# The gated recurrence moved between the last projection tiles, its norm squared on ScalarE and gated on VectorE

## The chip, the core and the metric

The kernel runs on one core of a Trainium2 chip. The metric is the device time of one execution in microseconds (us). Engines are named as in the profile: PE (TensorE; PEld is its weight load), DVE (VectorE), ACT (ScalarE), POOL (GpSimd), and SP, whose queue issues the loads. SBUF and PSUM are the on-chip memories; PSUM has eight banks of 512 fp32 columns.

## What is computed

One step of a one-layer streaming encoder on 1040 prompt tokens (16 meta tokens and 1024 frames) and 32 tokens of running streams, 1072 in all: an FFN with LayerNorm, a mixer, a second FFN. The mixer has two branches. One is a sparse attention: an indexer scores all keys, the 256 highest keys of each query are kept, then softmax. The other is a gated linear recurrence over four heads with a 128 x 128 state each. Shortened:

```
aq, ak, av, iq, ik, iw, bq, bf, bi, bg, ga, gb = split(h @ w_in)
oa   = sparse_attention(aq, ak, av, top-k of the indexer's scores (iq, ik, iw))
logf = log(lb + (1 - lb) * sigmoid(bf));  kk = (1 - lb) * sigmoid(-bf);  rq = silu(bq);  rv = bi
# recurrence, per head and block of tokens, b = cumsum(logf):
o    = tril(rq exp(b) (kk exp(-b))^T) rv + (rq exp(b)) S
S    = S exp(b_last) + (kk exp(b_last - b))^T rv
on   = o * rsqrt(mean(o^2) + eps) * g_norm;   ob = on * silu(bg)
h    = LN(alpha h + (sigmoid(ga) (oa @ wa) + sigmoid(gb) (ob @ wb)) @ wo)
```

All of it is fp32; a large product is done as three matmuls of split operands (`product3`: high x high, high x low, low x high).

## The kernel before

The program is a chain of stages. Activations lie transposed, features on the partitions and the 1072 tokens along the free side, in three chunks of 384, 384 and 304 columns.

**Index and project** (`index_and_project`). 43 tiles of 128 output columns of `w_in` are multiplied with h. A tile has three chunks, a chunk is 24 matmuls into one of four PSUM banks, and ACT drains it (`Projection.drain`). A tile's weights come by SP, ACT rounds them to the high part (`split_hi`, issued when the tile two earlier is drained), POOL subtracts (`split_lo`). While PE does so, DVE runs the indexer's search: after the scores, 31 rounds of counting and then the passes that mark the chosen keys (to L1272). DVE has nothing to do with the projections. The last 24 tiles (bi, bg, ga, gb) go through an SBUF buffer to a DRAM scratch (`spill`); aq, rq, ak, av and bf stay in SBUF.

**Mixers** (`mixers`), after a barrier. It starts with 21 transposes of ak, av and the cache, which DVE copies out of PSUM, and the split of the keys. Then each engine walks one list made by `pass_order`. Attention has ten blocks of eight heads, 80 units: seven blocks of 128 queries with 272, 400, ... 1040 keys, the 32 running tokens (288 keys), the first 128 frames (144 keys) and the 16 meta tokens. A unit n has the parts S (scores on PE, the distance penalty and row maximum on DVE, exp on ACT), T (PE turns the probabilities, ACT copies them out) and V (product with the values). S runs two units ahead. Q makes the queries of a block (ACT, DVE), X turns a block's output. The recurrence's parts are spread over the same list by a pace (`PACE`): g per head (`sums`: running sum of logf and its shifts, on DVE), e 32 times (exp of a quarter of a head on ACT into one of two buffers, a product on DVE), then for each of 13 blocks of 80 tokens and the 32 running tokens k, v (PE turns keys and values, ACT copies them), a (scores on PE, bound and mask on DVE), o (read-out on PE, copy on DVE), u (state update on PE, sum and product on DVE). At the end come four n, one per head: POOL squares the output, PE averages over the head's features with a matrix of ones (L1610), ACT takes the root (L1706), DVE the reciprocal and the product (L1863, L1865), POOL multiplies with the gate (L1482). Ahead of the list ACT makes the sigmoids and the logarithm (L1626 to L1635).

**Back** (`back`): output projections, LayerNorm, second FFN. It starts when the mixers' barrier is passed.

Within an engine the order is the program's. A wait on ACT or DVE holds everything behind it.

Of the kernel before, what the change touches and what calls it, by code (L numbers as in the profile page):

```python
# [22 lines left out]
P = 128  # L23
# [860 lines left out]
def score_columns():  # L884

    at, out = 0, {}
    for b in range(1, NB):
# [9 lines left out]
SPILLED = [(col, j, func) for col, m, func in ((C_BI, 4, ACT.Copy), (C_BG, 4, ACT.Silu), (C_GA, 8, ACT.Sigmoid),  # L897
                                               (C_GB, 8, ACT.Sigmoid)) for j in range(m)]
SP_BI, SP_BG, SP_GA, SP_GB = 0, 4, 8, 16


def index_and_project(c, block, dram, st, f, norm):
# [9 lines left out]
    tiles = [[(C_IQ + P * j, P, 0)] for j in range(4)] + [[(C_IK, P, 0)]]  # L912
    NI = len(tiles)
    tiles += [[(C_BF + P * j, P, 0)] for j in range(4)]
    tiles += [[(C_AQ + DH * j, DH, 0), (C_AQ + DH * (j + 4), DH, DH)] for j in range(4)]
    tiles += [[(C_AK, P, 0)], [(C_AV, P, 0)]]
    tiles += [[(C_BQ + P * j, P, 0)] for j in range(4)]
    NK = len(tiles)
    tiles += [[(col + P * j, P, 0)] for col, j, _ in SPILLED]
    NTL = len(tiles)  # L920
# [24 lines left out]
    k_hi, k_lo = c.k_hi, c.k_lo  # L945
    queries = QueryStack(c, "ix", c.q_stack, [(2 * j, 2 * j + 1) for j in range(4)])
# [6 lines left out]
    spilled = [sem(f"spilled{i}") for i in range(3)]  # L953
# [8 lines left out]
    index = {x[:3]: n for n, x in enumerate(units)}  # L962
    blocks = [(n, b, QB) for n, b in enumerate(range(1, NB))] + [(NB - 1, "s", DEC)]
# [6 lines left out]
    def _(sp):  # L970
# [17 lines left out]
        n_out = store_rows(sp, ki_tok, dram["new_kidx_p"], dram["new_kidx_s"], ki_out)  # L988
        for n in range(NI + 3, NTL):
            pr.load(sp, n)  # L990
        sp.wait_ge(ki_out, n_out)

    @block.gpsimd
    def _(pool):
        pr.split_lo(pool, 0)
        pr.split_lo(pool, 1)
        pr.split_lo(pool, 2)
        pr.split_lo(pool, 3)
        pool.iota(dist[:].bitcast(I32), [[-1, LP]], base=LP - P, channel_multiplier=1).then_inc(dist_set, 1)
        for n in range(4, NTL):  # L1000
            pr.split_lo(pool, n)

    @block.tensor
    def _(pe):
# [45 lines left out]
        for n in range(NI + EARLY // 3, NTL):  # L1050
            for i in range(3):
                pr.multiply(pe, n, i)

    @block.scalar
    def _(act):
# [31 lines left out]
        def drain(n, i):  # L1087
            m = n - NI
            if m < 4:
                pr.drain(act, n, i, c.y[:, m, :])  # L1090
            elif m < 8:
                pr.drain(act, n, i, c.aq[:, m - 4, :], scale=qscale[:, m - 4:m - 3])
            elif m < 10:
                pr.drain(act, n, i, c.ak if m == 8 else c.av)
            elif n < NK:
                pr.drain(act, n, i, c.rq[:, m - 10, :], ACT.Silu)
            else:
                m = n - NK
                pr.drain(act, n, i, c.y[:, 5 + m % 3, :], SPILLED[m][2])
# [12 lines left out]
        act.wait_ge(qs_set, 8)  # L1112
        for n in range(NI + EARLY // 3, NTL):
            m = n - NK
            if m == 0:
                act.wait_ge(ki_out, 48)
            if m >= 3:
                act.wait_ge(spilled[m % 3], 16 * (m // 3))
            for i in range(3):
                drain(n, i)  # L1120
            if m >= 0:
                pr.wait_drained(act, n)
                act.dma_start(c.spill[m], c.y[:, 5 + m % 3, :]).then_inc(spilled[m % 3], 16)
        for i in range(3):
            act.wait_ge(spilled[i], 16 * len(range(i, len(SPILLED), 3)))

    @block.vector
    def _(dve):
# [59 lines left out]

        dve.wait_ge(dist_set, 1)
# [67 lines left out]
        for n, b, rows in blocks:  # L1257
# [16 lines left out]
            settled()  # L1274


LOOK = 2
PACE = 1.22


def pass_order(att_blocks, n_rec):
# [9 lines left out]
    att = [("Q", 0)] + [("S", n) for n in range(LOOK)]  # L1291
    for n in range(units + 1):
# [978 lines left out]
```

## Time and profile before

| | us |
|---|---|
| median of 3 runs (lowest, highest) | 2945.52 (2942.11, 2946.82) |
| the profiled execution | 2947.6 |
| its span | 2945.9 |

| engine | busy us | share of the span |
|---|---|---|
| PE | 2730.8 | 93% |
| DVE | 1341.0 | 46% |
| ACT | 668.3 | 23% |
| POOL | 485.8 | 16% |

Times in the rows count from the span's start. The projections end near 1447 us, the mixers run from 1452 to 1862 us. PEclk is the clock that TensorE was granted, 1.00 for 2.4 GHz and 0.50 for 1.2 GHz; a value between is a stretch that had both. A matmul's duration overlaps the next one's, so what a run of them costs is read from the start of the first to the start of what follows.

### The profile page before, as it was taken

How to read it: one execution, taken by the hardware profiler on the slowest of the kernel's cores; microseconds unless marked ns; L12 is line 12 of the kernel's file. 1: busy time of each engine (PE TensorE's matmuls, PEld its weight loads, DVE VectorE, ACT ScalarE, POOL GpSimd, SP SyncE). 2: the span in 40 equal slices, each digit the busy share in tenths (PEclk: the TensorE clock that was granted, in tenths of full speed). 3: DMA queues.
4: the chain of work that ended last, by engine and by line, in shares of the span. 5: the costliest groups of instructions: out<-in, count | busy, mean ns of one | idle time of the engine just before them, and what ended most of it. 6: DMA issues, size and time to landing. Idle time of an engine off the chain costs nothing. (4 is left out here: it accounts for less than half of the span.)

```text
span 2945.9 us, 41396 instructions
## 1 busy us (share of the span) xinstructions
PE 2730.8 (93%) x16384; PEld 2628.7 (89%) x16384; DVE 1341.0 (46%) x2842; ACT 668.3 (23%) x1135; POOL 485.8 (16%) x175
## 2 busy tenths in 40 slices
PE   8999999999977999999779986799999999999996
PEld 7999999999967799999768974699799999999995
DVE  2333333333254689992165437455543333333335
ACT  3111111111143522221255533200421111111102
POOL 1122111111010011222100002111111111222212
PEclk9999999999988999999859987799999999999998
DMA  4111111111021011232200000522011111111101
GB/s 146 44 43 43 48 55 54 43 43 30 1 71 44 15 44 44 96 95 89 97 1 31 1 1 8 183 75 80 29 44 43 43 43 43 43 43 44 55 16 60
DMA packets 143708, 149.13 MB, mean 51 GB/s; under 512 B 19648, under 2 KB 130336, under 8 KB 143472
## 3 DMA queue, kind: packets, MB, share of 16 engines
q1 hardware_dynamic: 140144, 134.45, 14.8%
q10 hardware_dynamic: 3456, 13.17, 1.1%
q8 instruction: 76, 1.25, 0.2%
q14 instruction: 32, 0.26, 0.0%
HBM read 123.82 MB, written 23.79 MB: 50 GB/s over the span
## 5 line engine op out<-in xcount | busy, mean ns | idle before, releaser
L475 DVE TENSOR_TENSOR ffn_prod<-ffn_gate,ffn_psu 128x384 f32<-128x384 f32 x132 | 69.5, 527 | 799.9 <-ACT ffn_gate L385 793.6
L67 PE MATMUL ffn_psd<-ffn_hid_hi,ffn_dn_hi 128*128 128x384 f32 (+1 forms) x1056 | 353.9, 335 | 12.7 <-DVE y L500 10.9
L67 PE MATMUL ixp_ps<-h_hi,ixp_hi 128*128 128x384 f32 (+1 forms) x1032 | 339.9, 329 | 20.2 <-ACT y L877 11.5
L67 PE MATMUL ffn_psg<-h_hi,ffn_up_hi 128*128 128x384 f32 (+1 forms) x1056 | 346.4, 328 | 8.4 <-DVE ffn_up_lo L400 6.6
L500 DVE TENSOR_TENSOR y<-y,ffn_psd 128x384 f32<-128x384 f32 (+1 forms) x480 | 250.9, 526 | 217.2 <-PE ffn_psd L69 217.2
L385 ACT ACTIVATE ffn_gate<-ffn_psg 128x384 f32<-128x384 f32 x132 | 61.9, 469 | 1259.3 <-PE ffn_psu L69 1259.2
L67 PE MATMUL ffn_psu<-h_hi,ffn_up_hi 128*128 128x384 f32 (+1 forms) x1056 | 344.0, 326 | 0.0
L68 PE MATMUL ffn_psg<-h_lo,ffn_up_hi 128*128 128x384 f32 (+1 forms) x1056 | 343.9, 326 | 0.0
L69 PE MATMUL ffn_psd<-ffn_hid_hi,ffn_dn_lo 128*128 128x384 f32 (+1 forms) x1056 | 343.8, 326 | 0.0
L68 PE MATMUL ffn_psd<-ffn_hid_lo,ffn_dn_hi 128*128 128x384 f32 (+1 forms) x1056 | 343.7, 325 | 0.0
L69 PE MATMUL ffn_psg<-h_hi,ffn_up_lo 128*128 128x384 f32 (+1 forms) x1056 | 343.1, 325 | 0.0
L69 PE MATMUL ffn_psu<-h_hi,ffn_up_lo 128*128 128x384 f32 (+1 forms) x1056 | 343.0, 325 | 0.0
L68 PE MATMUL ffn_psu<-h_lo,ffn_up_hi 128*128 128x384 f32 (+1 forms) x1056 | 342.1, 324 | 0.0
L68 PE MATMUL ixp_ps<-h_lo,ixp_hi 128*128 128x384 f32 (+1 forms) x1032 | 337.9, 327 | 0.0
L69 PE MATMUL ixp_ps<-h_hi,ixp_lo 128*128 128x384 f32 (+1 forms) x1032 | 336.7, 326 | 0.0
L404 POOL TENSOR_TENSOR ffn_dn_lo<-ffn_dn_raw,ffn_dn_hi 128x2048 fp32r<-128x2048 f32 x22 | 101.8, 4627 | 912.5 <-ACT ffn_dn_hi L378 912.5
L400 POOL TENSOR_TENSOR ffn_up_lo<-ffn_up_raw,ffn_up_hi 128x2048 fp32r<-128x2048 f32 x42 | 194.7, 4637 | 331.6 <-ACT ffn_up_hi L372 331.6
L67 PEld LDWEIGHTS ffn_psd<-ffn_hid_hi,ffn_dn_hi 128*128 128x128 f32 x1056 | 198.3, 188 | 28.4 <-DVE y L500 17.7
L67 PEld LDWEIGHTS ixp_ps<-h_hi,ixp_hi 128*128 128x128 f32 x1032 | 195.9, 190 | 21.4 <-issue 12.0
L67 PEld LDWEIGHTS ffn_psg<-h_hi,ffn_up_hi 128*128 128x128 f32 x1056 | 199.2, 189 | 9.2 <-DVE ffn_up_lo L400 6.8
L858 POOL TENSOR_TENSOR ixp_lo<-ixp_raw,ixp_hi 128x1024 fp32r<-128x1024 f32 x43 | 105.7, 2460 | 575.4 <-ACT ixp_hi L853 575.4
L68 PEld LDWEIGHTS ffn_psg<-h_lo,ffn_up_hi 128*128 128x128 f32 x1056 | 199.5, 189 | 0.3
(299 smaller groups left out, 4995.5 us busy)
## 6 DMA issues: line engine op xcount, KB each, us to landing
ffn_dn_raw<-in_ffn_wd SPq DMA_DIRECT2D x22, 1024.0 KB, 4.9
ffn_up_raw<-in_ffn_wg SPq DMA_DIRECT2D x20, 1024.0 KB, 5.4
ffn_up_raw<-in_ffn_wu SPq DMA_DIRECT2D x20, 1024.0 KB, 7.8
ixp_raw<-in_w_in SPq DMA_DIRECT2D x39, 512.0 KB, 3.8
spill<-y ACTq DMA_DIRECT2D x24, 536.0 KB, 2.7
mo_sig<-spill SPq DMA_DIRECT2D x32, 192.0 KB, 3.8
y<-spill SPq DMA_DIRECT2D x2, 2144.0 KB, 8.3
y<-y_spill SPq DMA_DIRECT2D x1, 4288.0 KB, 15.0
```

The costliest lines, as they stand in the source:

```text
L67: pe.matmul(out, w_hi, x_hi, start=first, stop=False)
L68: pe.matmul(out, w_hi, x_lo, start=False, stop=False)
L69: return pe.matmul(out, w_lo, x_hi, start=False, stop=last)
L385: act.activation(self.gate[:, k % 2, 0:w], self.ps_gate[k % banks][:, 0:w], ACT.Silu).then_inc(self.silu_done, 1)
L400: eng.tensor_tensor(self.up_lo[:, j], self.up_view(j), self.up_hi[:, j].bitcast(F32), ALU.subtract).then_inc(self.up_lo_done, 1)
L404: pool.tensor_tensor(self.dn_lo[:], self.dn_raw[:], self.dn_hi[:].bitcast(F32), ALU.subtract).then_inc(self.dn_lo_done, 1)
L475: dve.tensor_tensor(self.prod[:, k % 2, 0:w], self.gate[:, k % 2, 0:w], self.ps_up[k % banks][:, 0:w], ALU.mult).then_inc(self.prod_done, 1)
L500: dve.tensor_tensor(y, y, self.ps_dn[o % 2][:, 0:w], ALU.add).then_inc(self.y_done, 1)
L858: pool.tensor_tensor(self.lo[b], self.raw[:, n % 2], self.hi[b].bitcast(F32), ALU.subtract).then_inc(self.lo_done, 1)
```

## The change

The recurrence with all its parts leaves `mixers` and becomes a class `Recurrence`, run inside `index_and_project`. Three things follow. The projected columns come in another order (`PROJECTED`): bf and rq ahead, aq now goes to the DRAM scratch and is loaded again in three parts at the mixers' start, bi stays in SBUF. ACT's sigmoids and logarithm (`decay`) come after tile 10, while DVE still searches; DVE's sums come after the search. The last eight tiles, 24 chunks, are dealt out by `step_order` between the recurrence's parts. In the mixers the list holds attention and, at every fourth unit from the third, one of twelve norm parts: q (squares, on ACT), n (root, reciprocal, product), g (gate, one DVE instruction for a head).

```diff
+STEP_TILES = 8
+def step_order(r):
+    chunks = [("P", n) for n in range(3 * STEP_TILES)]
+    out = []
+    for q in range(2 * r.NQ):
+        if q % 8 == 0:
+            out.append(chunks.pop(0))
+        out.append(("e", q))
+    out += [("G", 0), ("k", 0), chunks.pop(0), ("v", 0), chunks.pop(0), ("u", 0)]
+    for m in range(r.NRT):
+        more = m + 1 < r.NRT
+        out += [("k", m + 1)] * more + [("a", m)]
+        if chunks:
+            out.append(chunks.pop(0))
+        out += [("v", m + 1)] * more + [("o", m)]
+        if len(chunks) > r.NRT - m - 1:
+            out.append(chunks.pop(0))
+        out += [("u", m + 1)] * more
+    return out + chunks
...
+    def turn_keys(self, pe, n):
+        t0, w = self.span(n)
+        pe.wait_ge(self.scaled, 2 * self.NQ)
...
+    def grow_quarter(self, act, n):
+        h, t0 = self.quarters[n % self.NQ]
+        act.wait_ge(self.scanned, h + 1)
+        if n >= 2:
+            act.wait_ge(self.scaled, n - 1)
...
+        for n in range(NI + EARLY // 3, FIRST_STEP):
             for i in range(3):
                 pr.multiply(pe, n, i)
+        for what, n in order:
+            if what == "P":
+                pr.multiply(pe, FIRST_STEP + n // 3, n % 3)
+            elif what == "k":
+                rc.turn_keys(pe, n)
...
+            if n == NI + 5:
+                rc.decay(act, s_mm, len(units))
...
+        dve.memset(bit_f[:], 0.0).then_inc(searched, 1)
+        for h in range(BH):
+            rc.sums(dve, h)
+        for what, n in order:
+            if what == "e":
+                rc.scale_quarter(dve, n)
...
+    norm = [(what, h) for h in range(BH) for what in "qng"]
     for n in range(units + 1):
...
+        if n % 4 == 3 and norm:
+            att.append(norm.pop(0))
     att.append(("X", att_blocks - 1))
...
+                for part, spans in enumerate((((Q1, Q1 + QB),), ((Q1 + QB, LP),), ((LP, T), (0, Q1)))):
+                    for a, z in spans:
+                        sp.dma_start(c.aq[:, :, a:z], c.spill[SP["aq"]:SP["aq"] + 4, :, a:z].rearrange("n p t -> p n t")).then_inc(aq_in[part], 16)
...
+                    elif what == "q":
+                        for i, (t0, w) in enumerate(CHUNKS):
+                            if n >= 1:
+                                act.wait_ge(r_mm, 3 * n + i - 2)
+                            act.activation(sq[:, i, 0:w], rq[:, n, t0:t0 + w], ACT.Square).then_inc(sq_done, 1)
...
+                    elif what == "g":
+                        dve.wait_ge(on_done, 3 * n + 3)
+                        dve.tensor_tensor(rq[:, n, :], rq[:, n, :], gate[:, n, :], ALU.mult).then_inc(gated, 1)
```

Where PE's instructions stand. A projection chunk is 24 rows of L67, L68 and L69. In the kernel before the first turn of the recurrence's keys (rkv<-ident,kk) stands among attention's scores (s), turns (t) and value products (o), here with 656 keys:

```order
L1537 MATMUL mx_o<-mx_v_tok,mx_prob_t 128x64 x5
L1569 MATMUL mx_rkv<-ident,mx_kk 80x128 x4
L807 MATMUL mx_s<-mx_k_hi,mx_stack 128x328
L808 MATMUL mx_s<-mx_k_lo,mx_stack 128x328
L807 MATMUL mx_s<-mx_k_hi,mx_stack 128x328
```

In the changed kernel the same turn stands between the fourth and fifth chunk of the last eight tiles, and a step's first parts (u, k, a) stand together ahead of the next chunk:

```order
L69 MATMUL ixp_ps<-h_hi,ixp_lo 128x384
L1012 MATMUL ix_ps<-ident,rc_kk 80x128 x4
L67 MATMUL ixp_ps<-h_hi,ixp_hi 128x384
...
L69 MATMUL ixp_ps<-h_hi,ixp_lo 128x304
L1030 MATMUL ix_ps<-rc_rv_tok,rc_rk_tok 128x128 x4
L1012 MATMUL ix_ps<-ident,rc_kk 80x128 x4
L1038 MATMUL ix_ps<-rq,rc_kk 80x80 x4
L67 MATMUL ixp_ps<-h_hi,ixp_hi 128x384
```

What stands ahead of k is attention before, and four chunks of the last eight tiles now.

ACT in the last eight tiles. Before, a tile was three drains (L877), the rounding of the weights of a later tile (L853) and a store:

```order
L877 ACTIVATE y<-ixp_ps 128x384 x2
L877 ACTIVATE y<-ixp_ps 128x304
L853 ACTIVATE ixp_hi<-ixp_raw 128x1024
L1123 DMA spill<-y 128x1072
```

Changed, the 32 exponentials (L1081) stand among the drains of the first of these tiles, with a load of the function table at each crossing:

```order
L877 ACTIVATE ix_stage<-ixp_ps 128x384
L1081 ACT_TABLE_LOAD
L1081 ACTIVATE rc_grow<-y 128x268 x8
L877 ACT_TABLE_LOAD
L877 ACTIVATE ix_stage<-ixp_ps 128x384
L1081 ACT_TABLE_LOAD
L1081 ACTIVATE rc_grow<-y 128x268 x8
L877 ACT_TABLE_LOAD
L877 ACTIVATE ix_stage<-ixp_ps 128x304
L1429 DMA spill<-ix_stage 128x1072
L853 ACTIVATE ixp_hi<-ixp_raw 128x1024
L1081 ACT_TABLE_LOAD
```

DVE in the mixers. Before, a head's reciprocals (L1863) and products (L1865) stood at the end, among maxima (L1784, L1790) of blocks with 144 keys:

```order
L1790 TENSOR_SCALAR mx_peak_s,mx_bias<-mx_peak 128x1
L1863 RECIPROCAL y<-y 128x384
L1865 SCALAR_TENSOR_TENSOR rq<-rq,mx_gn,y 128x384
L1863 RECIPROCAL y<-y 128x384
L1865 SCALAR_TENSOR_TENSOR rq<-rq,mx_gn,y 128x384
L1863 RECIPROCAL y<-y 128x304
L1865 SCALAR_TENSOR_TENSOR rq<-rq,mx_gn,y 128x304
L1784 ISA mx_prob,mx_peak<-mx_s,dist_2423 128x144
```

Changed, the first head's stand in the second block:

```order
L1968 ISA mx_prob,mx_peak<-mx_s,score 128x400
L1968 ISA mx_peak 128x1
L1974 TENSOR_SCALAR mx_peak_s,mx_bias<-mx_peak 128x1
L2009 RECIPROCAL y<-y 128x384
L2011 SCALAR_TENSOR_TENSOR rq<-rq,mx_gn,y 128x384
L2009 RECIPROCAL y<-y 128x384
L2011 SCALAR_TENSOR_TENSOR rq<-rq,mx_gn,y 128x384
L2009 RECIPROCAL y<-y 128x304
L2011 SCALAR_TENSOR_TENSOR rq<-rq,mx_gn,y 128x304
L1968 ISA mx_prob,mx_peak<-mx_s,score 128x400
```

The other three heads stand in the same way after 12, 24 and 36 further units, in blocks with 528, 784 and 912 keys.

## Rows read from the trace of the kernel before

**Rows 1.** Stretches of 20 us, the whole core; the first line names the columns.

```profile
core 0: us, PE busy (x) PEld busy (x) DVE busy (x) ACT busy (x) POOL busy (x), PEclk, DMA share, GB/s
1420.00:1440.00 20.00, 20.00 (x126) 20.00 (x125) 0.00 (x0) 3.32 (x7) 2.41 (x1) 1.00 0.14 56
1520.00:1540.00 20.00, 17.93 (x70) 15.51 (x70) 11.18 (x40) 10.93 (x32) 0.00 (x0) 0.50 0.01 1
1560.00:1580.00 20.00, 16.92 (x127) 15.07 (x128) 9.31 (x39) 12.03 (x32) 0.00 (x0) 1.00 0.30 111
1740.00:1760.00 20.00, 15.44 (x102) 13.89 (x102) 4.53 (x16) 7.55 (x17) 0.00 (x0) 0.83 0.00 1
1800.00:1820.00 20.00, 6.53 (x21) 3.98 (x20) 17.22 (x17) 6.50 (x12) 9.57 (x12) 0.71 0.00 0
```

**Rows 2.** DVE in order of time (start us, us): search's end; one head's sums.

```profile
1347.15 0.45 DVE L1272 SCALAR_TENSOR_TENSOR score<-ix_scratch,ix_dist 32x288 f32<-32x288 f32 x1
...
1481.12 0.78 DVE L1750 TENSOR_SCALAR mx_kk<-mx_kk,mx_rest 128x1072 f32<-128x1072 f32 x1
...
1486.07 0.43 DVE L1784 CUSTOM_DVE_ANT_0 mx_prob<-mx_s,score 128x272 f32<-128x272 f32 x1
```

**Rows 3.** ACT in order of time: drains of tiles 34 and 42, one rounding.

```profile
1353.76 0.42 ACT L877 ACTIVATE y<-ixp_ps 128x304 f32<-128x304 f32 x1 [2.83 <-PE ixp_ps L69]
1354.08 1.05 ACT L853 ACTIVATE ixp_hi<-ixp_raw 128x1024 fp32r<-128x1024 f32 x1
...
1447.41 0.42 ACT L877 ACTIVATE y<-ixp_ps 128x304 f32<-128x304 f32 x1 [2.83 <-PE ixp_ps L69]
```

**Rows 4.** ACT in order of time: sigmoids and logarithms at the mixers' start.

```profile
1459.68 4.06 ACT L1631 ACTIVATE y<-y 128x1072 f32<-128x1072 f32 x4
1472.91 1.28 ACT L1635 ACT_TABLE_LOAD   x1 [9.16 <-DVE mx_rest L1742]
1474.20 4.80 ACT L1635 ACTIVATE y<-y,mx_lb,mx_rest 128x1072 f32<-128x1072 f32 x4
```

**Rows 5.** Groups by line and shape, 1420 to 1900 us: busy us, mean ns.

```profile
L1688 ACT ACTIVATE mx_grow<-y 128x268 f32<-128x268 f32 x32 | 13.1, 411 | 0.0
L1826 DVE TENSOR_TENSOR rq<-rq,mx_grow 128x268 f32<-128x268 f32 x16 | 7.0, 438 | 13.6 <-ACT mx_grow L1688 13.6
```

**Rows 6.** PE in order of time: scores and update of one recurrence step.

```profile
1580.26 0.73 PE L1585 MATMUL mx_rao<-rq,mx_kk 128*80 128x80 f32 x8
1580.83 1.40 PE L1537 MATMUL mx_o<-mx_v_tok,mx_prob_t 128*128 128x64 f32 x10
...
1587.98 1.05 PE L1578 MATMUL mx_ru<-mx_rv_tok,mx_rk_tok 80*128 80x128 f32 x8
1588.87 0.82 PE L1521 MATMUL mx_t<-ident,mx_prob 128*128 128x128 f32 x6
```

**Rows 7.** PE and ACT in order of time: first scores, then exps of units.

```profile
1472.72 0.56 PE L807 MATMUL mx_s<-mx_k_hi,mx_stack 128*128 128x272 f32 x1 [7.95 <-DVE mx_k_lo L1737]
...
1508.46 0.52 ACT L1644 ACTIVATE mx_prob<-mx_prob,mx_bias 128x272 f32<-128x272 f32 x1 [1.06 <-DVE mx_peak_s L1790]
...
1511.19 0.63 ACT L1644 ACTIVATE mx_prob<-mx_prob,mx_bias 128x400 f32<-128x400 f32 x1 [1.38 <-DVE mx_peak_s L1790]
...
1787.31 0.41 ACT L1644 ACTIVATE mx_prob<-mx_prob,mx_bias 128x144 f32<-128x144 f32 x1 [1.49 <-DVE mx_peak_s L1790]
...
1843.32 0.41 ACT L1644 ACTIVATE mx_prob<-mx_prob,mx_bias 128x144 f32<-128x144 f32 x1 [1.83 <-DVE mx_peak_s L1790]
...
1845.32 0.41 ACT L1644 ACTIVATE mx_prob<-mx_prob,mx_bias 128x144 f32<-128x144 f32 x1 [1.18 <-DVE mx_peak_s L1790]
...
1847.05 0.31 ACT L1644 ACTIVATE mx_prob<-mx_prob,mx_bias 16x16 f32<-16x16 f32 x1 [0.91 <-DVE mx_peak_s L1790]
```

**Rows 8.** DVE in order of time: a head's norm, from first reciprocal to next maximum.

```profile
1796.45 2.55 DVE L1863 RECIPROCAL y<-y 128x384 f32<-128x384 f32 x1 [2.72 <-ACT y L1706]
...
1805.23 0.30 DVE L1784 CUSTOM_DVE_ANT_0 mx_prob<-mx_s,dist 128x144 f32<-128x144 f32 x1
```

More of the change, by code:

```diff
@@ L1000, in _ @@
         for n in range(4, NTL):
+            if n == NI + 6:
+                pool.wait_ge(s_mm, len(units))
+                rc.constants(pool)
             pr.split_lo(pool, n)
@@ L1049, in _ @@
                 pr.multiply(pe, *early[n])
-        for n in range(NI + EARLY // 3, NTL):
+        for n in range(NI + EARLY // 3, FIRST_STEP):
             for i in range(3):
                 pr.multiply(pe, n, i)
+        for what, n in order:
[3 more added lines that the diff above has]
+                rc.turn_keys(pe, n)
+            elif what == "v":
+                rc.turn_values(pe, n, pr)
+            elif what == "u":
+                rc.update(pe, n)
+            elif what == "a":
+                rc.attend(pe, n)
+            elif what == "o":
+                rc.read(pe, n)
     @block.scalar
@@ L1087, in drain @@
         def drain(n, i):
[L1088 to L1096, printed above, removed]
-            else:
-                m = n - NK
-                pr.drain(act, n, i, c.y[:, 5 + m % 3, :], SPILLED[m][2])
+            kind, j = PROJECTED[n]
+            if kind == "f":
+                pr.drain(act, n, i, c.y[:, j, :])
+            elif kind in ("ak", "av"):
+                pr.drain(act, n, i, c.ak if kind == "ak" else c.av)
+            elif kind == "rq":
+                pr.drain(act, n, i, c.rq[:, j, :], ACT.Silu)
+            elif kind == "bi":
+                if i == 0:
+                    x = (j - 1) % 3
+                    if j >= 1:
+                        act.wait_ge(spilled[x], 16 * len(range(x, FIRST_SPILL[1] - FIRST_SPILL[0], 3)))
+                pr.drain(act, n, i, c.y[:, 4 + j, :])
+            else:
+                late = n >= FIRST_SPILL[2]
+                m = n - FIRST_SPILL[2 if late else 0]
+                out = stage[:, m % 2, :] if late else c.y[:, 5 + m % 3, :]
+                sent = late_spilled[m % 2] if late else spilled[m % 3]
+                if i == 0:
+                    if late and m == 0:
+                        act.wait_ge(searched, 1)
+                    if not late and m == 0:
+                        act.wait_ge(ki_out, 48)
+                        act.wait_ge(qs_set, 8)
+                    if m >= (2 if late else 3):
+                        act.wait_ge(sent, 16 * (m // (2 if late else 3)))
+                if kind == "aq":
+                    pr.drain(act, n, i, out, scale=qscale[:, j:j + 1])
+                else:
+                    pr.drain(act, n, i, out, ACT.Silu if kind == "bg" else ACT.Sigmoid)
+                if i == 2:
+                    pr.wait_drained(act, n)
+                    act.dma_start(c.spill[SP[kind] + j], out).then_inc(sent, 16)
             if i == 2 and n + 2 < NTL:
@@ L1615, in make_stack @@
                     q0, m = blocks[b][0:2]
+                    for part in range(3 if b >= NB - 1 else 2 if b else 1):
+                        act.wait_ge(aq_in[part], 32 if part == 2 else 16)
                     if b >= 2:
```

511 lines of the change are left out of this document (262 added, 249 removed).

## The prediction, made before the changed kernel ran

> **What bounds the kernel now.** I read the table of engines first: PE is busy 93% of the span, so a moved piece of work can only pay by closing PE's idle time, or the time in which PE is busy at the low clock. Then the stretches of 20 us [rows 1]. In the projections PE has no gap, its clock is full and DVE stands still: that is what the change wants to use. DVE's search ends at 1347.6 [rows 2], the last drain is at 1447.4 [rows 3], so DVE is free for 100 us. In the mixers it is otherwise: at 1520 PE is busy 17.93 of 20 us but at clock 0.50, at 1740 busy 15.44 at 0.83, at 1800 only 6.53 while DVE has 17.22. Last the order of time of the mixers' start and end [rows 7] and of the norm [rows 8]: from the first score to the second block's first exp 38.5 us pass, and the last nine units of attention spread over 59.7 us because DVE is at the norm. These two ends are what can be won; everything between them is PE work that has to be done in one stage or the other.
>
> **Projection stage, in the order of its new parts.** (1) Logarithm of the decay on ACT after tile 10. A tile is 93.65 / 8 = 11.71 us of PE [rows 3], which over 384 + 384 + 304 columns is 4.19, 4.19 and 3.32 for its chunks. ACT has, before its next drain: rounding 1.05 [rows 3], three table loads of 1.28, twice four sigmoids at 4.06, four logarithms at 4.80 [rows 4], in sum 17.8, and some 1.5 for the drain and the small constants: 19.3 us. The four banks let PE compute four chunks meanwhile, 3 x 4.19 + 3.32 = 15.9. Behind the decay on ACT's queue stand the drains that free the banks: **+3.5**.
>
> (2) The growth phase. PE may turn the first keys (k of step 0) only when all 32 products are done, and ahead of that stand just four chunks. These chunks now begin near 1353.8 + 3.5 = 1357 and end near 1373. DVE can't start its sums before the search is over: 1347.6 + 4 x 4.95 [rows 2] = 1367.4, with semaphores 1368.2. Then 32 pairs of exp and product, 0.411 and 0.438 each [rows 5]. Two buffers let the two engines overlap, but each product waits for its exp and each exp for the product two earlier; with 0.12 for the semaphores half of 0.97, that is 0.485 a pair, 15.5 in all. Three times ACT must cross to a drain and back: two loads of 1.28 and a drain near 0.49, 3.05, once with a rounding of 1.05 as well, together 10.3. So k starts near 1394, and PE stands 21 us; behind it on PE's queue wait all later chunks, so nothing hides this: **+21.5**. If exp and product overlap fully (0.44 a pair) and half of the crossings lies under DVE's work, it is 15; if the pairs do not overlap (0.97 a pair) it is 37. The first buffer is free at once and both engines have short work, which is nearest to overlap; I keep the middle. After such a stop the clock will be down for a while, as it is after the gap ahead of the mixers' first scores (PE idle ahead of them, later 0.50) [rows 1, 7]: one chunk at half clock, **+3**, between 0 and 8.
>
> (3) The steps. Scores are 8 records of 0.071, the update 8 of 0.111 [rows 6]; turns of keys and values, the read-out (two products) make 24 more like the update. 32 x 0.111 + 8 x 0.071 = 4.1 us a step, x 14 = **+57.5**. Their copies (ACT, DVE) are meant to lie under chunks of 3.3 to 4.2 us. The values' copy stands on ACT behind drains, and in every tile behind a rounding of 1.05; where the update waits for it I take **+3** in all, from 0 to the 18 of a rival below. Sum of the stage: 3.5 + 21.5 + 3 + 57.5 + 3 = **+88.5**.
>
> **Mixers.** (4) Start. From first score to the exp of unit 8 it is 38.5 us [rows 7], since DVE makes four heads' sums (19.8) and a part of the growth between. Without them I take 4.8 to the first maximum and the unit cadence of 2.73 from there: 18.5. **−20**. (5) PE no longer does the steps: 57.5, and more where the clock is 0.83 [rows 1]: **−61**, against which **+4** where these matmuls only filled gaps of attention (PE is idle 4.6 of 20 us at 1740). (6) The end: 59.7 us, 8 units at 2.0 remain, and 4.5 of it was already counted in (5): 59.7 − 16 − 4.5 = **−39.2**. (7) The norm is not gone, it now stands in blocks of 400, 528, 784 and 912 keys. A head holds DVE 2.72 (waiting for ACT's root) and 8.78, 11.5 us [rows 8], and behind it in DVE's queue stand the maxima of the next units, so ACT has no exp, PE no turns. PE has scores two units ahead and the turns and values of one, about one unit's work of 2.75 (the cadence of [rows 7]): 4 x (11.5 − 2.75) = **+35**; with two units hidden 24, with none 46. (8) After each of the four gaps the clock falls, as it is 0.71 at 1800: **+6**. The squares on ACT (1072 columns in three passes, one pass of that length takes 4.06 / 4 = 1.02 [rows 4], so 1.7 at most) and the gate on DVE (the same columns, between a sum's pass of 0.78 [rows 2] and four products of 0.438 [rows 5], I take 1.3) are short parts in queues with room: **+4**. Sum: −20 − 61 + 4 − 39.2 + 35 + 6 + 4 = **−71.2**.
>
> The rest costs nothing that I can find: aq's way to DRAM and back takes bi's place in the same number of stores, and its first part lies before the mixers' first queries beside the 21 transposes; if it came late the start would move by its length, a few us. POOL loses squares and gate, under which nothing waited but the norm itself.
>
> **Total.** +88.5 − 71.2 = +17.3 on the profiled 2947.6 gives 2964.9; the median lies 2.1 below that execution: **2963**.
>
> **Rivals.** A, not slower: the low clock of the blocks with 272 to 528 keys is lifted. From the first exp at 1508 to about 1560 PE runs at 0.50 with 17.93 of 20 busy, and in the next stretch at 1.00 with 16.92 [rows 1, 7]. If the norm's averages (dense matmuls, the first of them now after the seventh unit) or the missing recurrence raise it there, PE's 17.9 become 9 and DVE's 11.2 with its waits, some 13 of 20, bound the units: 52 x 7 / 20 = 18 to 20 less, **2944**. For it: the clock did rise at 1560 without any visible gap's end. Against it: each norm opens a gap of its own, and gaps come before low clocks in the rows. It decides if half or more of these units are at full clock.
>
> B: every step opens a gap on PE. A hand-over from DVE leaves ACT idle 1.06 to 1.83 us in attention [rows 7]; a step has four of them, and one chunk of 4.19 must cover two, with ACT in a rounding at times. With 1.3 us a step, 14 x 1.3 = 18: **2981**.
>
> D: after the second norm the low clock stays through the block of 656 keys; where 16.92 of 20 were at full clock [rows 1] 20 us become 38: +18, **2981**.
>
> C: each change of function table costs twice what a load shows. The first logarithm begins 1.29 us after its load's start, but ahead of this load ACT was idle 9.16 us [rows 4], under which a wait for the engine to run empty would lie unseen. Nine loads lie on the way (three in the decay, six at the crossings); 9 x 1.3 = 12 more: **2975**. The Trainium skill, "ScalarE: Activation LUTs", section "What ACT_TABLE_LOAD costs", says so: about 1283 ns for the load and about 1380 ns for a drain, and with its figure the sum, an estimate, would be 2975 as well. By that rule, the trace agrees on the load and is silent on the drain.
>
> E: the change doesn't do what it says, for instance the norm is still the last thing of the mixers. The order of instructions speaks against it.
>
> **How the numbers follow.** The forecast, 2952 to 2973, has 0.56; A 0.20; B 0.11; D 0.07; C 0.05; E, or a gain that I don't see, 0.01. About 0.2%, 5.9 us, is what a measurement of this kernel can tell from no change: 2939.6 and 2951.4 are the bounds. A is a little more often within them than below (0.10 faster, 0.10 same); the low edge of the forecast, where the growth phase takes 15 and the norm 24, adds 0.05 to no change; E 0.01 to faster. Faster 0.11, same 0.15, slower 0.74. The range 2942 to 2981 takes in A's middle and B's and D's, and leaves out A's lower part and what adds up above.
>
> **What the changed profile would show.** Right: a wait of some 21 us on PE before the first turn of keys (L1012) for DVE's products; a gap of 3 to 4 us near 1080 behind the decay; the projections' end near 1536 in place of 1447; PE near solid in the last tiles; the mixers about 340 us long in place of 411; four gaps of 5 to 10 us on PE there, each at a norm's reciprocals (L2009), with PEclk falling behind each; no idle end. Wrong on (2): exps running against products closely enough that k waits under 12 us, or sums that start late. Wrong on (7): PE busy through the reciprocals. A shows as PEclk near 1.00 in the mixers' first 80 us, B as PE idle of a microsecond at L1030 or L1051 in every step, D as 0.50 in the fourth block, C as 2.6 us between the exp before and the drain after a load. The forecast fails as a whole if the mixers come out under 320 us or the projections' end lies under 1520.

## The result, and the profile after

| | before | changed |
|---|---|---|
| median us (lowest, highest) | 2944.20 (2942.11, 2946.82), 4 runs | 2996.24 (2991.30, 2998.67), 4 runs |
| ratio to before, 95% interval | | 1.0174 (1.0157, 1.0192) |
| the profiled execution, its span | 2947.6, 2945.9 | 2991.3, 2989.6 |

The changed kernel is 52 us slower, where 17 were forecast. Its profiled execution is the fastest of its four runs, so the two traces differ by 43.7 us only; the forecast was a sum against the traced execution of before, and that is what the parts below are held against.

Both ends of the mixers were won as forecast, and more was paid in between. The stretches of the mixers, by groups of attention's blocks: start and 272 keys; 400 and 528; 656 to 912; 1040 and the running tokens (288); 144 and 16 keys. First the kernel before (the columns are those of [rows 1]):

```profile
core 0: us, PE busy (x) PEld busy (x) DVE busy (x) ACT busy (x) POOL busy (x), PEclk, DMA share, GB/s
1455.90:1511.20 55.30, 26.70 (x94) 19.38 (x94) 43.38 (x115) 26.53 (x53) 0.00 (x0) 0.50 0.19 63
1511.20:1573.60 62.40, 57.78 (x274) 51.02 (x273) 32.95 (x127) 33.80 (x99) 0.00 (x0) 0.62 0.05 18
1573.60:1688.90 115.30, 113.23 (x894) 107.07 (x893) 60.10 (x203) 60.34 (x145) 0.00 (x0) 0.97 0.03 11
1688.90:1787.30 98.40, 84.09 (x629) 74.78 (x628) 37.00 (x133) 35.45 (x90) 0.00 (x0) 0.91 0.01 4
1787.30:1861.30 74.00, 43.76 (x172) 31.40 (x171) 44.54 (x97) 25.83 (x82) 20.32 (x24) 0.60 0.02 4
```

The changed kernel:

```profile
1548.40:1584.90 36.50, 26.59 (x93) 19.35 (x94) 20.74 (x72) 11.30 (x36) 0.00 (x0) 0.50 0.39 134
1584.90:1664.00 79.10, 63.91 (x271) 55.50 (x271) 40.42 (x115) 34.47 (x84) 0.00 (x0) 0.59 0.00 1
1664.00:1784.00 120.00, 100.01 (x609) 90.48 (x607) 58.73 (x178) 61.73 (x143) 0.00 (x0) 0.81 0.00 1
1784.00:1873.90 89.90, 78.61 (x396) 66.61 (x395) 22.94 (x105) 30.68 (x81) 0.00 (x0) 0.63 0.00 1
1873.90:1904.40 30.50, 28.61 (x133) 21.87 (x131) 9.17 (x70) 12.06 (x64) 0.00 (x0) 0.50 0.00 1
```

The start is 18.8 us shorter and the end 43.5. The three groups between are 276.1 us before and 289.0 now, though PE no longer has the recurrence's 58 us of matmuls in them (start to next start) and makes 1276 records in place of 1797. In the fourth group PEclk went from 0.91 to 0.63: PE makes 396 records in 78.6 us, where it made 629 in 84.1. There is no norm in this group.

In the projections' stage, PE's waits between 1370 and 1410, in the changed kernel (engine, line, who is waited for, us, times, longest):

```profile
PE ix_ps L1012 <- DVE rc_kk L1142: 27.2, 1, 27.2
```

On DVE, in order of time, the end of the search (0.45 us at 1347.15 in [rows 2]) and one instruction of the second head's sums, the copy at 1360.51; the first head's copy of the same line and shape took 0.17:

```profile
1351.86 0.45 DVE L1609 SCALAR_TENSOR_TENSOR score<-ix_scratch,ix_dist 32x288 f32<-32x288 f32 x1
1352.37 0.06 DVE L1612 MEMSET ix_bit_f<- 128x1 f32 x1
...
1355.56 0.17 DVE L1123 COPY rc_bmid<-y 128x13 f32<-128x13 f32 x1
...
1360.51 2.19 DVE L1123 COPY rc_bmid<-y 128x13 f32<-128x13 f32 x1
```

ACT at one of the three crossings, answering to [rows 4, 5]:

```profile
1377.22 0.78 ACT L1081 ACTIVATE rc_grow<-y 128x268 f32<-128x268 f32 x2 [0.21 <-DVE rq L1142]
1378.02 1.28 ACT L877 ACT_TABLE_LOAD   x1
1379.31 0.49 ACT L877 ACTIVATE ix_stage<-ixp_ps 128x384 f32<-128x384 f32 x1
1379.82 1.28 ACT L1081 ACT_TABLE_LOAD   x1
1381.11 0.74 ACT L1081 ACTIVATE rc_grow<-y 128x268 f32<-128x268 f32 x2
```

And PE's longest waits in the blocks with 400 to 912 keys. They hold the four stops of the norm: three of 7.0, 7.4 and 6.5 us for score banks that the delayed maxima hold (the fourth wait of that line is 0.4), and one of 6.9 for probabilities:

```profile
PE mx_s L807 <- DVE mx_peak L1968: 21.3, 4, 7.4
PE mx_o L1823 <- ACT mx_prob_t L1894: 6.9, 1, 6.9
```

The granted clock before, during and after the third of these stops (columns as above):

```profile
1700.00:1705.50 5.50, 5.50 (x34) 4.48 (x33) 1.99 (x1) 5.45 (x10) 0.00 (x0) 1.00 0.00 0
1705.50:1712.90 7.40, 0.04 (x1) 0.00 (x0) 7.29 (x9) 0.08 (x1) 0.00 (x0) 0.71 0.00 0
1712.90:1729.00 16.10, 15.44 (x62) 14.12 (x63) 6.94 (x25) 7.67 (x18) 0.00 (x0) 0.50 0.00 1
```

It falls within the stop and stays down for some 16 us of matmuls behind it. The second and the fourth stop look the same, with 18 and 6 us at 0.50 behind them.

### The profile page after: what moved, and what is told of

Read it like the earlier page. It is cut to its first block and busy times, and to the rows that moved or that the text cites. A ratio compares the mean times of both kernels' runs of the same rounds, so it can differ in the third digit from the quotient of the medians.

```text
span 2989.6 us, 41403 instructions
## 1 busy us (share of the span) xinstructions
PE 2767.2 (93%) x16384; PEld 2661.3 (89%) x16384; DVE 1356.6 (45%) x2846; ACT 694.8 (23%) x1161; POOL 466.3 (16%) x151
## 5 line engine op out<-in xcount | busy, mean ns | idle before, releaser
L67 PE MATMUL ffn_psd<-ffn_hid_hi,ffn_dn_hi 128*128 128x384 f32 (+1 forms) x1056 | 354.2, 335 | 12.7 <-DVE y L500 10.9
L67 PE MATMUL ixp_ps<-h_hi,ixp_hi 128*128 128x384 f32 (+1 forms) x1032 | 343.3, 333 | 23.8 <-ACT y L877 11.5
L67 PE MATMUL ffn_psg<-h_hi,ffn_up_hi 128*128 128x384 f32 (+1 forms) x1056 | 346.2, 328 | 8.4 <-DVE ffn_up_lo L400 6.6
L67 PE MATMUL ffn_psu<-h_hi,ffn_up_hi 128*128 128x384 f32 (+1 forms) x1056 | 344.0, 326 | 0.0
L69 PE MATMUL ffn_psd<-ffn_hid_hi,ffn_dn_lo 128*128 128x384 f32 (+1 forms) x1056 | 343.8, 326 | 0.0
L68 PE MATMUL ffn_psd<-ffn_hid_lo,ffn_dn_hi 128*128 128x384 f32 (+1 forms) x1056 | 343.7, 325 | 0.0
L68 PE MATMUL ffn_psg<-h_lo,ffn_up_hi 128*128 128x384 f32 (+1 forms) x1056 | 343.6, 325 | 0.0
L69 PE MATMUL ffn_psg<-h_hi,ffn_up_lo 128*128 128x384 f32 (+1 forms) x1056 | 343.0, 325 | 0.0
L69 PE MATMUL ffn_psu<-h_hi,ffn_up_lo 128*128 128x384 f32 (+1 forms) x1056 | 343.0, 325 | 0.0
L68 PE MATMUL ffn_psu<-h_lo,ffn_up_hi 128*128 128x384 f32 (+1 forms) x1056 | 342.1, 324 | 0.0
L68 PE MATMUL ixp_ps<-h_lo,ixp_hi 128*128 128x384 f32 (+1 forms) x1032 | 339.4, 329 | 0.0
L69 PE MATMUL ixp_ps<-h_hi,ixp_lo 128*128 128x384 f32 (+1 forms) x1032 | 338.5, 328 | 0.0
L67 PEld LDWEIGHTS ffn_psd<-ffn_hid_hi,ffn_dn_hi 128*128 128x128 f32 x1056 | 198.3, 188 | 28.4 <-DVE y L500 18.2
L67 PEld LDWEIGHTS ixp_ps<-h_hi,ixp_hi 128*128 128x128 f32 x1032 | 197.6, 191 | 25.3 <-issue 15.6
L67 PEld LDWEIGHTS ffn_psg<-h_hi,ffn_up_hi 128*128 128x128 f32 x1056 | 199.0, 188 | 9.3 <-DVE ffn_up_lo L400 6.9
L68 PEld LDWEIGHTS ffn_psg<-h_lo,ffn_up_hi 128*128 128x128 f32 x1056 | 199.4, 189 | 0.3
```

The costliest lines, as they stand in the source:

```text
L67: pe.matmul(out, w_hi, x_hi, start=first, stop=False)
L68: pe.matmul(out, w_hi, x_lo, start=False, stop=False)
L69: return pe.matmul(out, w_lo, x_hi, start=False, stop=last)
```

## The experiments

The kernels ran in four groups, each with its own runs of the kernel before, whose medians were 2947.23, 2946.64, 2949.22 and 2947.39 us. Since these differ by more than some effects, ratios to before are the safer measure; 0.1% is 2.9 us. The changed kernel stands at 1.0174.

### 1. Does the norm drag the clock down, or does the missing recurrence?

The norm left out, in `pass_order`:

```
-    norm = [(what, h) for h in range(BH) for what in "qng"]
+    norm = []
```

> The changed kernel without the norm: neither squares, means, roots, reciprocals, products nor gates of the recurrence's output. Theory CLOCK (the recurrence's matmuls between attention's kept PE's clock up, and without them the late blocks fall to 0.50 whatever the norm does): only the norm's own stops go, four of about 7 us and some low clock behind them, 28 to 38 us in all, so about 2960 to 2968, and the block of 1040 keys, where no norm stands in the changed kernel either, keeps its 62 us with some 45 of them at clock 0.50. Rival NORM (the stops of the norm drag the clock down for the whole of the mixers): the stops and the 56 us of added low clock go together, 28 + 28 us or more, so 2940 or less, and the block of 1040 keys comes near 50 us at full clock.

2946.54 us, ratio 0.9999 (0.9989, 1.0009): 1.75% or some 51 us less than the changed kernel, far more than CLOCK's 28 to 38 and somewhat under NORM's 56 or more. But the trace divides it. The same five groups:

```profile
1548.20:1584.70 36.50, 26.61 (x94) 19.40 (x94) 20.76 (x72) 10.26 (x34) 0.00 (x0) 0.50 0.39 135
1584.70:1644.10 59.40, 58.47 (x264) 52.59 (x264) 22.09 (x100) 24.80 (x70) 0.00 (x0) 0.56 0.00 1
1644.10:1730.90 86.80, 79.77 (x591) 72.97 (x591) 39.00 (x166) 51.41 (x128) 0.00 (x0) 1.00 0.01 1
1730.90:1819.00 88.10, 76.11 (x396) 64.25 (x394) 21.83 (x104) 30.40 (x80) 0.00 (x0) 0.66 0.00 1
1819.00:1849.60 30.60, 28.71 (x134) 21.93 (x132) 9.19 (x72) 12.14 (x64) 0.00 (x0) 0.50 0.00 1
```

In the blocks where the norm stood, 53 us are gone: PE's idle time (length less busy time of the second and third group) fell by 27 of them, from 35.2 to 8.0; the rest is the norm's matmuls and the clock, which is 1.00 in the third group in place of 0.81. In the second group it is low either way (0.56 without the norm, 0.59 with it), so there the norm costs its stops and its own work and pulls nothing down. In the fourth group little changed: 88.1 against 89.9 us at 0.66 against 0.63. So each theory holds in its place: the norm's stops pull the clock down in the blocks of 656 to 912 keys, and from the block of 1040 keys on it is down without any norm.

### 2. Is it the missing dense work that lowers the clock in the late blocks?

Seven unused matmuls in each of the units 48 to 63, behind T on PE (shortened):

```
+                        if 48 <= n < 64:
+                            for x in range(7):
+                                pe.matmul(ps_n[n % 2][:, 0:P], ones[:], ones[:], start=True, stop=True)
```

> The changed kernel with seven more matmuls of 128 x 128 in each of the 16 units of the blocks with 1040 keys and of the running tokens, their result unused: 112 x 0.222 = 25 us of PE work at full clock, about as much as the recurrence had in these blocks before (12.2 and 12.6). Theory CLOCK: the dense work lifts the clock in these blocks and pays for itself in good part; the two blocks, 89.8 us together now and 98.5 before, grow by less than 12 us, total below 3008. Rival NORM, or any in which these matmuls don't change the clock: PE is busy through most of these blocks, so they grow by 25 us or more (up to 50 where the clock stays at 0.50): 3018 to 3045.

3002.95 us, ratio 1.0179 (1.0151, 1.0208), against 1.0174. The fourth group is now

```profile
1783.80:1884.80 101.00, 85.58 (x593) 76.64 (x592) 22.96 (x107) 30.45 (x80) 0.00 (x0) 0.88 0.00 1
```

197 more matmul records (a matmul of this kind is two records, and some are missing) and 7 us more of PE's busy time, 11 us more of length, and the clock at 0.88. That is under the 12 us of CLOCK. The whole run moved by 0.05%, with intervals of 0.2 and 0.3%, so it can't tell these 11 us from none. In these two blocks, then, 25 us of added dense work cost 11, and the recurrence's 25 us, taken away, gave back 8.5 (98.4 against 89.9): the clock made up for more than half of either.

### 3. The wait for the growth factors

`quarters` by head (four of rq and four of kk for each), and DVE makes the next head's sums ahead of each eight products:

```
-        for h in range(BH):
-            rc.sums(dve, h)
+        rc.sums(dve, 0)
         for what, n in order:
             if what == "e":
+                if n % 8 == 0 and n // 8 + 1 < BH:
+                    rc.sums(dve, n // 8 + 1)
                 rc.scale_quarter(dve, n)
```

> The changed kernel with the growth factors taken head by head, each head's eight exponentials and products behind the sums of the next head, so that ACT's exponentials and table loads lie under DVE's sums. Theory: the 27.2 us in which PE waits for the products ahead of the first turn of keys is the chain sums, then exp and product in turn with three crossings; with the chain overlapped the products end near 1386 in place of 1401, PE waits about 11 us, total 15 us less, near 2981. Rival (ACT's table loads and drains set the phase, not the order): the wait stays over 22 us and the total within 5 us.

2986.89 us, ratio 1.0139 (1.0115, 1.0162), some 10 us less than the changed kernel where 15 were expected; the two profiled executions differ by 6.7. PE's wait:

```profile
PE ix_ps L1012 <- DVE rc_kk L1142: 21.0, 1, 21.0
```

It fell by 6.2 us, which is between the two expectations. Of the crossings one is still bare (the last head has no sums behind it), and the sums of the second and of the fourth head are each held up by one copy of 2.2 us. Three chunks more ahead of the first turn of keys (`AHEAD` is 3):

```
+    out += [chunks.pop(0) for _ in range(AHEAD)]
     out += [("G", 0), ("k", 0), chunks.pop(0), ("v", 0), chunks.pop(0), ("u", 0)]
```

> The growth factors head by head as in the run before, and three more chunks ahead of the first turn of keys (seven in place of four; fewer are left between the steps). The products ended at 1395 there and PE waited 21.0 us. Theory: a chunk is 4 us of PE, and ACT drains one bank behind each eight exponentials, so PE can do the three within the wait: it falls by 10 to 12 us, and the steps lose little: 9 to 12 us less than the run with the growth head by head (2987), some 2976. Rival (the chunks taken from the steps were what hid their hand-overs): as much comes back as gaps of PE between the steps, total within 4 us of 2987.

2977.65 us, ratio 1.0111 (1.0091, 1.0131), and the wait is

```profile
PE ix_ps L1014 <- DVE rc_kk L1144: 8.3, 1, 8.3
```

As expected. The projections end at 1524.9 in place of 1541.2; the 16.3 us are the 18.9 less of waiting, nearly whole, so fewer chunks between the steps cost next to nothing, which also speaks against rival B.

### 4. The norm's engines alone

The kernel before with squares on ACT and the gate on DVE, at the old place (short form; the POOL part falls away):

```
+                        if n == 0:
+                            act.wait_ge(out_done, NRT)
+                            square(0)
+                        if n + 1 < BH:
+                            square(n + 1)
...
+                        dve.wait_ge(on_done, 3 * n + 3)
+                        dve.tensor_tensor(rq[:, n, :], rq[:, n, :], gate[:, n, :], ALU.mult).then_inc(gated, 1)
```

> The kernel before with only the norm's engines changed: squares on ACT, gate on DVE, at the old place. Theory: at the end of the mixers DVE sets the pace with 8.8 us a head, the gate adds about 1.3 a head to it, the squares lie beside: 3 to 8 us more than before, 2947 to 2952. Rival (the hand-overs to POOL cost more than that): as much less, 2938 or below.

2958.47 us, ratio 1.0040 (1.0029, 1.0052): 12 us slower, more than either expectation. The gate stands behind the product and ahead of the next maximum on DVE:

```profile
1809.58 0.54 DVE L1861 SCALAR_TENSOR_TENSOR rq<-rq,mx_gn,y 128x304 f32<-128x304 f32 x1
1810.15 1.27 DVE L1864 TENSOR_TENSOR rq<-rq,y 128x1072 f32<-128x1072 f32 x1
1811.34 0.30 DVE L1780 CUSTOM_DVE_ANT_0 mx_prob<-mx_s,dist 128x144 f32<-128x144 f32 x1
```

That is 5.1 us for four heads. The squares alone:

> The kernel before with the norm's squares alone on ACT, the gate left on GpSimd. The gate on DVE took 1.27 us a head in the run with both (5 us in all), behind which the maxima of the next units wait; both together cost 11 us. If the rest is the squares (ACT makes the next head's ahead of this head's roots, so roots and products wait): 2951 to 2955, 4 to 6 us slower than before. If it is all the gate: within 2 us of before.

2954.64 us, ratio 1.0023 (1.0010, 1.0036): 7 us for the squares, which leaves 5 for the gate. The two intervals overlap, so the times alone hardly divide them, but the traces agree: the last group of blocks takes 74.0 us before, 79.7 with the squares moved and 84.5 with both. Where the norm stands at the end, both moves lose.

### 5. Where the norm stands

All twelve parts behind units 66 to 77:

```
-        if n % 4 == 3 and norm:
+        if n >= 66 and norm:
```

> The changed kernel with the norm's twelve parts one after the other behind units 66 to 77, in the blocks of 144 and 16 keys, where the kernel before had its norm. Theory (a head's 11.5 us of DVE cost what of them attention on PE can't cover, and the late blocks have the least of it): the blocks with 400 to 912 keys fall to the lengths without a norm (146 us together in place of 199), the end of the mixers grows by 50 us, as the norm costs at the end of the kernel before with its engines changed (70.3 against 16.3): total within 5 us of the changed kernel. Rival (in the blocks of 400 to 912 keys most of the cost is the low clock behind each stop, and the end, which is at the low clock anyway, does not pay it a second time): 15 us or more less than the changed kernel.

2983.08 us, ratio 1.0124 (1.0104, 1.0144): 13 to 15 us less than the changed kernel (by medians and by ratios), which is about the rival's size and not the theory's. The last group of blocks grew by 41 us (30.5 to 71.2), those with 400 to 912 keys lost 53:

```profile
1823.20:1894.40 71.20, 42.60 (x157) 29.19 (x155) 48.31 (x98) 33.27 (x96) 0.00 (x0) 0.52 0.00 1
```

Its clock was 0.50 before the norm came there, so it had nothing to lose. Then DVE's share in pieces, one chunk of a head at a time, PE's means and ACT's roots a part ahead; a part behind every second unit up to the 47th, and behind every unit from the 44th to the 67th:

```
-    norm = [(what, h) for h in range(BH) for what in "qng"]
+    norm = [x for h in range(BH) for x in (("q", h), ("n", h), ("d", (h, 0)), ("d", (h, 1)), ("d", (h, 2)), ("g", h))]
```

> The changed kernel with DVE's share of the norm in three pieces a head (reciprocal and product of one chunk, some 3.2 us) and PE's and ACT's share one part ahead of them, a part behind every second unit up to the 47th. Theory PIECES: a piece is about as long as PE's work on one unit, so the four stops of 7 us go, and with them the low clock behind them: of the 50 us that the norm costs (from the run without it) at most 20 stay, total 2955 to 2968. Rival WORK (the norm's cost is its instructions on DVE and ACT wherever they stand, ACT's table loads among them): 2980 or more.

> The same pieces, a part behind every unit from the 44th to the 67th, in the blocks of 1040 keys and the running tokens above all, where DVE is busy 10 of 60 us and a unit lasts 3.5 to 7.7 us. Theory PIECES: nearly all of it is hidden there, 0 to 12 us over the run without a norm, total 2947 to 2960. Rival WORK: 2980 or more. Between them: 2960 to 2975, if the low clock of these blocks gets longer.

2977.26 us, ratio 1.0107 (1.0087, 1.0127), and 2965.05, ratio 1.0075 (1.0055, 1.0094). Against the run without a norm that is 1.1% or 32 us, and 0.76% or 22 us. Neither theory was right for the first. The second came where its expectation had put the case between the theories, and for the reason given there: the low clock of its late blocks got longer (84 us of 107 at 0.50, where the run without a norm has 59 of 88). Pieces in the early blocks still leave stops of 3.5 to 4.3 us and the clock behind them; in the late blocks they cost less, but not nothing.

### 6. The low clock at the mixers' start

Unused matmuls of the identity with itself, one behind each transpose, 24 ahead of the first scores; and in the second kernel, whose edit this is (shortened), seven more in each of the first 24 units:

```
+START, SPANS, PER = (1, 24), [(0, 24)], 7
...
                     elif what == "T":
                         turn(n)
+                        if any(a <= n < z for a, z in SPANS):
+                            fill(PER)
```

> The changed kernel with unused matmuls of 128 x 128 where PE waits at the mixers' start: one behind each of the transposes and 24 ahead of the first scores, 45 x 0.222 = 10 us of PE work at full clock, most of it inside waits. Theory START (PE comes into attention at the low clock because it stood for 7 and 8 us, and attention with 272 to 528 keys does not lift it): if it comes in at full clock it keeps it, and the 68 us that these blocks spend at 0.50 without or with a norm's stop shrink by 15 to 30 us: 2968 to 2982. Rival (these blocks fall to the low clock by their own matmuls, whatever the clock at their start): nothing gained, 2996 to 3008.

> The same with seven more matmuls in each of the first 24 units (168 x 0.222 = 37 us at full clock, 75 at half). Theory START or CLOCK (dense work lifts the clock in these blocks as the recurrence did in the later ones): the blocks with 272, 400 and 528 keys run mostly at 1.00 and the run costs 10 us less to 15 us more than the one before. Rival: they stay at 0.50 and the work costs 37 to 75 us more.

2997.30 us, ratio 1.0166 (1.0145, 1.0186), and 2991.79, ratio 1.0152 (1.0132, 1.0172). The first falls out for the rival: start and block of 272 keys have a mean clock of 0.74, but it is back at 0.50 before that block ends, and nothing is gained. The second has 37 us more PE work and takes 4 us less, a difference that the intervals don't clear; what they do show is that the work did not cost its 37. Its first two groups:

```profile
1546.70:1585.00 38.30, 35.50 (x268) 33.65 (x268) 21.06 (x72) 11.67 (x36) 0.00 (x0) 0.91 0.39 131
1585.00:1665.20 80.20, 69.66 (x497) 64.56 (x496) 40.38 (x114) 34.56 (x83) 0.00 (x0) 0.89 0.00 1
```

Twice the matmul records (765 against 364) in 3 us more, at 0.91 and 0.89 in place of 0.50 and 0.59. So the low clock of these blocks comes from what PE is given there; what about attention's own matmuls earns it, these runs do not show.

### 7. Together

The edits of 3 and the late pieces of 5:

> Three edits together: growth factors head by head, seven chunks ahead of the first turn of keys, the norm in pieces in the blocks from 1040 keys on. If they add up: 2996 - 19 (2977.65 against 2996) - 31 (2965 against 2996) = 2946, the time of the kernel before. Rival: the norm's pieces interact with the shorter stage, over 2955.

2945.06 us, ratio 0.9996 (0.9980, 1.0012): they add up, to the time of the kernel before. With unused matmuls at the start and in all units from the 48th on:

> The same with the unused matmuls at the mixers' start and seven in each unit from the 48th to the last (224 x 0.222 = 50 us of PE work at full clock). Theory CLOCK: they lift the late blocks' clock and pay for themselves, within 8 us of the run without them, below it if attention's own matmuls gain more than the fillers take. Rival: 25 us or more above it.

2967.76 us, ratio 1.0054 (1.0035, 1.0073): 17 us by the ratios, 23 by the medians, for 60 of added work. It lies between the two expectations. The blocks of 1040 keys and the running tokens keep their length (105.7 us against 105.3), those of 144 and 16 keys grow by 16: there the work is more than the clock gives back. Then fewer, in the first 24 units only, four, two, and four there and in units 48 to 63:

> The three edits together (2945), with the unused matmuls at the mixers' start and four (0.9 us at full clock) in each of the first 24 units. Theory CLOCK: with seven a unit of 272 keys took 2.6 us, PE busy throughout at 1.00; with four PE has 2.0 us a unit there and some 2.7 in the blocks of 400 and 528 keys, so these two shrink from 61 us to 45 or 50 and the run is 8 to 16 us faster than without: 2929 to 2937. Rival (four a unit are too few to lift the clock): 21 us of added PE work at full clock, 43 at half: 2966 or more.

> The same with two a unit. If the clock holds with two, 2925 to 2935; if not, the work costs 11 to 22 us: 2956 to 2967.

> Four a unit in the first 24 units and in the 16 of the blocks of 1040 keys and the running tokens. Seven a unit there left the two blocks as long as without (105.7 against 105.3 us) with the clock at 1.00 for most of them. Theory CLOCK: four cost less, 3 to 8 us below the run with the early ones alone. Rival: as long or longer, since these blocks wait for DVE and ACT, not PE.

| | median us | ratio to before (95%) |
|---|---|---|
| without | 2945.06 | 0.9996 (0.9980, 1.0012) |
| four, early | 2942.91 | 0.9983 (0.9970, 0.9996) |
| two, early | 2934.13 | 0.9961 (0.9946, 0.9975) |
| four, early and late | 2937.25 | 0.9982 (0.9967, 0.9997) |

The version with two is 0.4% faster than the kernel before and 2.1% faster than the changed one. Its first two groups:

```profile
1531.50:1564.80 33.30, 29.05 (x208) 27.00 (x208) 21.07 (x72) 10.13 (x34) 0.00 (x0) 0.90 0.43 146
1564.80:1616.00 51.20, 45.51 (x325) 41.82 (x324) 21.94 (x100) 24.82 (x71) 0.00 (x0) 0.93 0.00 1
```

and of the version without:

```profile
1531.80:1568.30 36.50, 26.62 (x94) 19.38 (x94) 20.75 (x72) 10.15 (x34) 0.00 (x0) 0.50 0.40 132
1568.30:1629.50 61.20, 60.27 (x264) 54.29 (x263) 22.08 (x100) 24.77 (x70) 0.00 (x0) 0.54 0.00 1
```

13 us less for these 24 units. Two a unit came as expected; four brought less than the 8 to 16 us forecast (in the traces 5.6 in these units). Whether late fillers help beyond the early ones stays open: 2937.25 against 2942.91 in medians, but 0.9982 against 0.9983 in ratios. Whether two are better than four is near the edge of the intervals.

## Why the prediction was wrong

It named the direction and most mechanisms; the size was out by more than its range. By its own steps, in the traces:

| step | forecast | measured |
|---|---|---|
| (1) decay, PE's stop | +3.5 | 3.37 from 1087.9 to 1091.3, then 2.9 us of matmuls at clock 0.50 |
| (2) wait for the products | +21.5, clock +3 | 27.2; the clock was 0.50 from 1377.5 to 1404.8, of it 3.7 us under matmuls |
| (3) steps, with their waits | +60.5 | 60.5: the 140.1 us from k to the end, less 77.8 for 20 chunks and 1.9 for the low clock |
| projections' end | 1447.4 + 88.5 | 1541.2, +93.8 |
| (4) mixers' start | −20 | −18.8 |
| (6) end, with (5)'s 4.5 | −43.7 | −43.5 |
| (5) recurrence off PE, the blocks between | −52.5 | −41.8 |
| (7), (8) norm inside attention | +45 | +55 |
| mixers in all | −71.2 | −49.4 |

**(2) was mis-sized by 5.7 us**, and not in the part that looked uncertain. Two exps begin 0.99 us after the two before, 0.49 a pair as forecast, and over the crossings it is 3.5, 5.0 and 3.5 us from product to product, where 3.5, 4.6 and 3.5 were in the sum. What came late was the search, which ended at 1352.3 and not 1347.6. In the search loop three small instructions took 2.1 to 2.3 us where their like take 0.2 (at 1051, 1062 and 1093), and a copy in the sums took 2.19 in place of 0.17. The trace of the kernel before has none of these. What held them isn't settled; the three of the loop stand at the same places in six further traces of the changed program. I had taken DVE's timetable over from the old program unchanged.

**(5) failed as a step.** I priced the removal of 57 us of PE work at its duration, with 4 back for gaps. The trace had the counter-evidence: [rows 1] show PE at 0.50 where attention is alone and at 1.00 once the recurrence stands between. The blocks of 656 to 912 keys lost 28.5 of the 32.7 us that its matmuls had there (run without a norm against before), but those of 1040 keys and the running tokens lost 10.3 of 24.8, since their clock fell from 0.91 to 0.66. The run with fillers in these blocks put the same amount of work back and shows that its absence is the cause: the clock came back to 0.88, and 25 us of work lengthened the blocks by 11.

**(7) and (8) had the mechanism right and the shares wrong.** The stops of PE were 27.7 us where I had 35, some seven for a head. PE's idle time grew by 27 in all; the rest of the 53 in those blocks is 8.4 of the norm's own matmuls, which I had left out, and some 17 of slower matmuls, where I had 6. The half-clock time of the blocks with 400 to 912 keys is 110 us in the changed kernel and 52 without the norm; 45 of these 58 us are in the blocks from 656 keys on. The sum, +45 against +55, hid that.

**(4) came out right by luck.** 4.8 us and the eight units of 2.73 up to the exp of unit 8 are 26.6, not the 18.5 of the sum; that would have been −12. In the changed kernel this stretch took 19.7: the first exp began 1.5 us behind the first score and the fourth 2.9 later, and the next five intervals averaged 3.05.

(2), (5) and the norm's terms (7) and (8) are 5 + 11 + 10 of the 26.4 us between +17.3 and +43.7. The median lies 4.9 us above the profiled execution, where I had taken it 2.1 below as in the kernel before; together that is the 33 us between 2963 and 2996.

**The rivals.** A said that the blocks of 272 to 528 keys would run at full clock; they did not, the two groups stayed at 0.50 and 0.59, and the norm's means did not lift them. (Its exp at 1508 is that of unit 7; the first is at 1480, and the clock of the kernel before is 0.50 from its start of the mixers on.) Its price, 18 to 20 us, was of the right order: the two fillers a unit lift these blocks and bring 13 us with their own cost paid. D (low clock through the block of 656 keys) came in part: 13.9 of the block's 32.7 us are at 0.50. The clock was the lever that decided, and I put it at 6 us in the sum and into rivals that only asked where it would be better or worse in one block, not what it would be wherever the recurrence is taken out. B failed: from the first turn of keys to the projections' end the trace has two gaps of 0.3 us at L1030 and no other over that, and steps with fewer chunks between them cost next to nothing. C failed: behind an exp that ended at 1378.00 the load starts at 1378.02 and the copy out of PSUM (L877) 1.29 later, so with ACT busy right up to it there is no second wait. The Trainium skill, "ScalarE: Activation LUTs", section "What ACT_TABLE_LOAD costs", gives about 1283 ns for the load, which these rows bear out, and about 1380 ns of drain with it, which they don't show.

E did not come: the parts moved as the order says.

## What to carry to other kernels

Work taken off a busy engine gives back its duration only if the clock at which that engine does the rest stays; where two kinds of work are interleaved, look at the granted clock of the stretches in which one of them is alone before pricing its removal. Where the clock is full, a stop costs its length and then the slow matmuls behind it, so a long instruction group on another engine is better cut in pieces, or put where the clock is down already. And a timetable of another engine that a new dependence hangs on (here the end of the search) should get a margin of its own, since in the changed program it came 5 us later for a reason that stays open.

## What the runs showed of the hardware

TensorE was busy 58.5 of 59.4 us at a mean granted clock of 0.56, most of it the level of 1.2 GHz (blocks of 400 and 528 keys, run without a norm). The same blocks came to 0.89 and 0.93, most of it 2.4 GHz, when seven and two more matmuls stood in each unit; with two, and the norm in late pieces, they ended sooner in spite of the added work, in 51.2 us for 61.2. The dense fillers ahead of the first unit did not carry over: the mean clock was 0.91 up to the first scores and 0.59 from there to the end of the first block.

The clock's timing also varies from run to run. In two traces with the same code for the block of 1040 keys and the running tokens (four and two early fillers) this stretch took 106 and 94.5 us, with 83 and 51 us at 0.50, and single executions of the kernels with ten runs lie 14 to 18 us apart. Comparisons of single executions mean little at that size.
